# Paired projections from seven block products, with their sums on VectorE, in a hybrid RG-LRU / HGRN2 / MoE layer

## What is computed

```python
def token_mixer(h, s_lru, s_hgrn, row_len, lb, w_in, ...):
    proj = h @ w_in                                   # (tokens x 1024) @ (1024 x 3584)
    xr, gr, q_raw, ff, fb, iv, og = jnp.split(proj, ...)     # seven groups of 512 columns
    y_lru = rmsnorm(h_f + h_b, norm_lru) * jax.nn.gelu(gr)   # two RG-LRU scans of conv(xr)
    y_hg, new_hgrn = hgrn2(q_raw, ff, fb, iv, og, lb, norm_hgrn, s_hgrn)
    y = jnp.concatenate([y_lru, y_hg], axis=-1) @ w_out

def hgrn2(...):                       # four heads of 128 channels, two directions each
    q = silu(q_raw) * DK ** -0.5;  v = i_raw
    # direction: logf = log(lb + (1-lb) sigmoid(f)), k = (1-lb) sigmoid(-f); gated chunks with a state
    o = rmsnorm(o_f + o_b, gain) * silu(g_raw)
```

## Time and profile before

| | us |
|---|---|
| median of three runs | 959.01 |
| the profiled execution | 958.34 |
| its span | 956.6 |
| TensorE busy | 928.8 (97%) |
| VectorE busy | 516.9 (54%) |
| ScalarE busy | 289.7 (30%) |
| GpSimd busy | 101.2 (11%) |

### The profile page before, as it was taken

The page is one execution under the profiler, slowest core; times in us unless marked ns, Lnnn a source line. Parts: engine busy times, 40 slices in busy tenths (PEclk is TensorE's granted clock), DMA queues, the critical chain, the costliest instruction groups (busy, mean ns, idle before and its releaser), DMA issues.

```text
span 956.6 us, 19027 instructions
## 1 busy us (share of the span) xinstructions
PE 928.8 (97%) x8298; PEld 423.3 (44%) x8298; DVE 516.9 (54%) x1269; ACT 289.7 (30%) x507; POOL 101.2 (11%) x115
## 2 busy tenths in 40 slices
PE   5999999999999999999999999999999999999996
PEld 4555756768667554463222222222222223333332
DVE  4487667663654743764464461752636516444096
ACT  5137756564653824323020100200202002010103
POOL 3200010000000022112102002011020110100100
PEclk9999999999999999999999999999999999999999
DMA  9991014404029443168999999999999999999993
GB/s 333 334 386 52 2 55 157 160 5 176 10 92 367 174 164 150 66 240 323 403 399 404 408 416 408 415 401 413 418 405 413 405 413 425 401 426 413 412 380 122
DMA packets 52930, 276.15 MB, mean 289 GB/s; under 512 B 4400, under 2 KB 12752, under 8 KB 39920
## 3 DMA queue, kind: packets, MB, share of 16 engines
q1 hardware_dynamic: 45744, 253.77, 66.1%
q0 software_dynamic: 5584, 15.89, 5.7%
q10 hardware_dynamic: 1520, 5.28, 1.4%
HBM read 261.91 MB, written 13.01 MB: 287 GB/s over the span
## 4 chain that ended last, share of the span: by engine, by line
PE 79%; DMA 8%; DVE 5%; ACT 3%; issue 3%; POOL 0%; SPq 0%; POOLq 0%; DVEq 0%; ACTq 0%
PE pa L699 44%; PE p L699 34%; DMA ring<-in_w_up_dram 3%; DMA reg_e<-in_w_up_dram 3%; DMA ring<-in_w_ada_dram 1%; ACT reg_c L1374 1%; ACT L1374 1%; ACT reg_d L1374 1%; DMA reg_c<-h_rows,row_s 0%; ACT reg_b L1374 0%; DVE reg_a L2246 0%; DVE reg_b L1867 0%; PE p L854 0%; DVE reg_a L2241 0%; DVE reg_b L1838 0%
## 5 line engine op out<-in xcount | busy, mean ns | idle before, releaser
L699 PE MATMUL pa<-ring,reg_b 128*32 128x512 f32 (+1 forms) x1696 | 250.0, 593 | 0.7 <-DMA ring<-in_w_up_dram 0.5
L699 PE MATMUL p<-ring,reg_b 128*16 128x512 f32 (+1 forms) x1920 | 215.3, 592 | 1.1 <-issue 1.1
L699 PE MATMUL pa<-reg_a,ring 128*128 128x512 f32 (+1 forms) x640 | 191.2, 453 | 2.2 <-DVE reg_a L1730 1.5
L699 PEld LDWEIGHTS pa<-ring,reg_b 128*32 128x32 f32 (+1 forms) x1696 | 82.5, 117 | 143.7 <-issue 142.6
L699 PEld LDWEIGHTS pa<-reg_a,ring 128*128 128x128 f32 x640 | 98.3, 191 | 80.1 <-issue 79.9
L699 PEld LDWEIGHTS p<-ring,reg_b 128*16 128x16 f32 (+1 forms) x1920 | 63.9, 102 | 143.9 <-issue 143.9
L2142 DVE STREAM_TRANSPOSE reg_b<-reg_b 32x128 f32<-32x128 f32 x384 | 116.3, 303 | 5.9
L2158 DVE TENSOR_TENSOR reg_b<-reg_b,pa 128x512 f32<-128x512 f32 x16 | 11.0, 686 | 146.7 <-PE pa L699 146.4
L1374 ACT ACTIVATE reg_b<-pa 128x512 f32<-128x512 f32 (+1 forms) x20 | 12.4, 619 | 239.8 <-PE pa L699 239.8
L1374 ACT ACTIVATE reg_b<-reg_d,x_mod 128x128 f32<-128x128 f32 (+1 forms) x112 | 39.4, 440 | 140.7 <-PE p L699 140.7
L1374 ACT ACT_TABLE_LOAD x57 | 73.1, 1283 | 4.6 <-issue 2.8
(11 more groups left out here) (335 smaller groups left out, 937.4 us busy)
## 6 DMA issues: line engine op xcount, KB each, us to landing
ring<-in_w_gate_dram SPq DMA_DIRECT2D x25, 2048.0 KB, 21.1
ring<-in_w_down_dram SPq DMA_DIRECT2D x24, 2048.0 KB, 24.1
ring<-in_w_up_dram SPq DMA_DIRECT2D x22, 2048.0 KB, 21.5
ring<-in_w_ada_dram SPq DMA_DIRECT2D x8, 2048.0 KB, 8.5
ring<-in_w_in_dram SPq DMA_DIRECT2D x6, 2048.0 KB, 19.9
ring<-in_w_ada_dram SPq DMA_DIRECT2D x8, 1024.0 KB, 12.8
reg_a<-in_w_up_dram SPq DMA_DIRECT2D x4, 2048.0 KB, 20.3
reg_a<-in_w_gate_dram SPq DMA_DIRECT2D x3, 2048.0 KB, 18.1
```

Of the source, the lines that this page charges most:

```text
L699: return nc.tensor.matmul(out, lhsT, rhs, start=start, stop=stop, **kw)
```

## The change

Items 0 and 1 of the last two of each `FILL[u]`, u = 0 to 5, become a pair in `TWOS`: (Q, OG), (FF, FB) of heads 1, 2 and 3. A pair's product, [1024 x 256] weights with 640 tokens, is cut in 2 x 2 blocks on each side (512 rows; 320 tokens, `HALF`), and computed by seven block products (a scheme of Strassen and Winograd) instead of eight: each `product` is four matmuls of 320 columns.

- Token sums `x_sum`: four [128 x 1280] sums, once, by GpSimd. Weight sums `weight_sums`: four [128 x 512] sums for each pair by VectorE, two pairs ahead.
- The products go to four PSUM banks. ScalarE copies two of them (`two_copy`); seven adds of 320 columns on VectorE join them (`two_sum`, step 0 in every unit between `less` and `weigh`; steps 1 to 4, six adds, after `reach` in even units and after the state copy in odd ones). In even units ScalarE then runs Silu over both results, in place.
- TensorE's order in a unit is new (`unit_projections`); `EARLY` is now V of head 1; V of heads 2 and 3 comes first in its unit. `head_norm` moves behind the fourth product.
- `w_in` arrives in cells of 1024 x 128 (0.5 MB, runs of 512 bytes) in the order of their use; the sums take the place of two ring slots. Some slots are freed later. A few buffers and semaphores are renamed or moved; GpSimd's store of the LRU state comes behind its sums.

```diff
 
 
 LOADS = [(("ada", 0), 0), (("in", IN_XR), 4), (("ada", 1), 1), (("ada", 2), 2), (("ada", 3), 3),
-         (("in", IN_Q), 5), (("in", IN_OG), 0), (("in", IN_FF), 1), (("in", IN_FB), 2), (("in", IN_V), 3)]
+         (("head", 5), 5), (("head", 0), 0), (("head", 1), 1), (("sums", 0), 2), (("sums", 1), 3)]
 LOADS += [(("ada", c), 4) for c in range(4, 12)] + [(("in", IN_GR), 4), (("out", 0), 5), (("out", 1), 0)]
...
+    FILL += [[(IN_Q, _h), (IN_OG, _h)], ([(IN_V, _h)] if _h > 1 else []) + [(IN_FF, _h), (IN_FB, _h)]]
+TWOS = [fill[-2:] for fill in FILL]
 FILL += [[(IN_GR, 0), (IN_GR, 1)], [(IN_GR, 2), (IN_GR, 3)]]
-HEAD0 = [(IN_Q, 0), (IN_OG, 0), (IN_FF, 0), (IN_FB, 0), (IN_V, 0)]
-
-EARLY = FILL[1].pop(0)
+
...
+        mixing = ring[:, 2:4, :, :].rearrange("p s k n -> p (s k n)")
+        x_sum = [mixing[:, m * 4 * HALF:(m + 1) * 4 * HALF].rearrange("p (k t) -> p k t", k=4) for m in range(4)]
+        w_sum = [[mixing[:, 16 * HALF + (3 * b + m) * 512:16 * HALF + (3 * b + m + 1) * 512].rearrange("p (k n) -> p k n", k=4)
+                  for m in range(3)] for b in range(2)]
+        x_quarter = [[hT[:, 4 * kh:4 * kh + 4, HALF * th:HALF * (th + 1)] for kh in range(2)] for th in range(2)]
+        banks = [pa[n // 2][:, 512 * (n % 2):512 * (n % 2) + HALF] for n in range(4)]
...
+            def cell_load(g, h):
+
+                src = w_in_v[:, :, g * 512 + h * P:g * 512 + (h + 1) * P]
+                sp_eng.dma_start(w_cell((g, h)), src).then_inc(loaded[CELL_BY[(g, h)][0]], 16)
...
+                cell_load(g, 0)
+            sp_eng.wait_ge(freed[0], 1)
+            cell_load(IN_V, 0)
+            cell_load(IN_Q, 1)
+            cell_load(IN_OG, 1)
+            cell_load(IN_V, 1)
+            sp_eng.wait_ge(freed[1], 1)
+            cell_load(IN_FF, 1)
+            cell_load(IN_FB, 1)
+            cell_load(IN_Q, 2)
+            cell_load(IN_OG, 2)
+            whole_load("ada", 4)
+            sp_eng.wait_ge(full, 3)
+            cell_load(IN_FF, 2)
+            sp_eng.wait_ge(full, 4)
+            cell_load(IN_FB, 2)
+            sp_eng.wait_ge(full, 5)
+            cell_load(IN_V, 2)
+            sp_eng.wait_ge(full, 6)
+            cell_load(IN_V, 3)
+            whole_load("ada", 5)
+            whole_load("ada", 6)
+            sp_eng.wait_ge(two_ps, 7)
+            sp_eng.wait_ge(*cells_by((IN_V, 3)))
+            cell_load(IN_Q, 3)
+            cell_load(IN_OG, 3)
...
+            pool.wait_ge(freed[2], 1)
+            pool.wait_ge(freed[3], 1)
+            nc.gpsimd.tensor_tensor(x_sum[0], x_quarter[1][0], x_quarter[1][1], ALU.add).then_inc(mixed, 1)
+            nc.gpsimd.tensor_tensor(x_sum[2], x_quarter[0][0], x_quarter[1][0], ALU.subtract).then_inc(mixed, 1)
+            pool.wait_ge(mixed, 2)
+            nc.gpsimd.tensor_tensor(x_sum[1], x_sum[0], x_quarter[0][0], ALU.subtract).then_inc(mixed, 1)
+            pool.wait_ge(mixed, 3)
+            nc.gpsimd.tensor_tensor(x_sum[3], x_quarter[0][1], x_sum[1], ALU.subtract).then_inc(mixed, 1)
...
+            def product(i, bank, w, x):
+                for k in range(4):
+                    r = mm(banks[bank], w[:, k, :], x[:, k, :], k == 0, k == 3)
+                r.then_inc(two_ps, 1)
+
+            def two_start(i):
+
+                one, two = TWOS[i]
+                for g, h in (one, two):
+                    pe.wait_ge(*cells_by((g, h)))
+                pe.wait_ge(empty[0], (USE[one] + 1) // 2)
+                product(i, 0, w_cell(one)[:, 0:4, :], x_quarter[0][0])
+                pe.wait_ge(empty[1], USE[one] // 2)
+                pe.wait_ge(mixed, 4)
+                pe.wait_ge(two_add, weights_by(i))
+                product(i, 2, w_sum[i % 2][0], x_sum[0])
+
+            def two_middle(i):
+
+                product(i, 1, w_cell(TWOS[i][0])[:, 4:8, :], x_quarter[0][1])
+
+            def two_second(i):
+
+                product(i, 3, w_sum[i % 2][1], x_sum[1])
+
+            def two_third(i):
+
+                pe.wait_ge(two_cp, copied_by(i) + 2)
+                product(i, 2, w_cell(TWOS[i][1])[:, 4:8, :], x_sum[3])
+                product(i, 0, w_cell(TWOS[i][1])[:, 0:4, :], x_sum[2])
+
+            def two_last(i):
+
+                pe.wait_ge(two_add, joined_by(i) + 1)
+                product(i, 3, w_sum[i % 2][2], x_quarter[1][1])
+                pe.sem_inc(full, 2)
+                for at, slots in ((2, (1,)), (4, (5,)), (5, (0, 2, 3))):
+                    if i == at:
+                        pe.wait_ge(two_ps, 7 * i + 7)
+                        for s in slots:
...
+            def unit_projections(u):
+                if len(FILL[u]) > 2:
+                    project(FILL[u][0])
+                if u > 0:
+                    two_start(u)
+                if u == 1 or u == 3 or u == 5:
+                    pe.wait_ge(sc_done, NSC * u)
+                    ada_sum(ADA_UNIT[u])
+                two_middle(u)
                 if u == 0:
                     pe.wait_ge(ln_log, 1)
-                elif u in ADA_UNIT:
-                    pe.wait_ge(sc_done, NSC * u)
-                if u in ADA_UNIT:
                     ada_sum(ADA_UNIT[u])
-                project_prompt(fill[0])
+                two_second(u)
+                if u == 2 or u == 4:
+                    head_norm(u // 2 - 1)
+                two_third(u)
+                if u == 2 or u == 4:
+                    turn_k(u)
+                    two_last(u)
+                    return
+                if u <= 1:
+                    ada_sum(ADA_UNIT[u] + 1)
+                    turn_k(u)
+                    two_last(u)
+                else:
+                    two_last(u)
+                    ada_sum(ADA_UNIT[u] + 1)
+                    turn_k(u)
+                ada_turn(ADA_UNIT[u])
...
+            def two_copy(i, step):
+                (one_a, one_b), (two_a, two_b) = two_out(TWOS[i][0]), two_out(TWOS[i][1])
+                act.wait_ge(two_ps, 7 * i + 1 + step)
+                A((one_a, two_b)[step], banks[2 * step], ACT.Copy).then_inc(two_cp, 1)
...
                 chain(A(kk, f, ACT.Sigmoid, scale=-1.0))
                 A(lf, W[6], ACT.Ln, bias=lb[:, 4 * d + h:4 * d + h + 1], scale=oml[:, 4 * d + h:4 * d + h + 1]).then_inc(lfk, 1)
+                if len(fill) > 2:
+                    projected(fill[0])
+                if u < len(TWOS):
+                    two_copy(u, 0)
+                    two_copy(u, 1)
...
+                elif d == 0:
+                    for item in fill:
+                        n = USE[item]
+                        act.wait_ge(empty[n % 2], n // 2 + 1)
+                    for item in fill:
+                        dst = yT[:, LT + item[1], :] if item[0] == IN_OG else raw[item[1] % 2][2]
+                        A(dst, dst, ACT.Silu).then_inc(two_cp, 1)
...
+            def weight_sums(i):
+                one, two = TWOS[i]
+                for item in (one, two):
+                    dve.wait_ge(*cells_by(item))
+                if i >= 2:
+                    dve.wait_ge(two_ps, 7 * (i - 1))
+                t1, t2, t4 = w_sum[i % 2]
+                a, b, at = w_cell(one), w_cell(two), weights_by(i) - 4
+                V.tensor_tensor(t1, b[:, 0:4, :], a[:, 0:4, :], ALU.subtract).then_inc(two_add, 1)
+                V.tensor_tensor(b[:, 0:4, :], b[:, 4:8, :], b[:, 0:4, :], ALU.subtract).then_inc(two_add, 1)
+                dve.wait_ge(two_add, at + 1)
+                V.tensor_tensor(t2, b[:, 4:8, :], t1, ALU.subtract).then_inc(two_add, 1)
+                dve.wait_ge(two_add, at + 3)
+                V.tensor_tensor(t4, a[:, 4:8, :], t2, ALU.subtract).then_inc(two_add, 1)
+
...
             V.memset(reg_e[:, 0:2 * T], 0.0).then_inc(zeroed, 1)
 
             for j in range(1, LT):
...
+            def two_sum(i, step):
+                (one_a, one_b), (two_a, two_b) = two_out(TWOS[i][0]), two_out(TWOS[i][1])
+                at = joined_by(i)
+                if step == 4:
+                    for dst, other in ((two_a, two_b), (two_b, one_b)):
+                        dve.wait_ge(two_add, at + (4 if dst is two_a else 5))
+                        V.tensor_tensor(dst, dst, other, ALU.add).then_inc(two_add, 1)
+                after, dst, src, bank = ((4, two_a, one_a, 3), (3, one_a, one_a, 1), (6, one_b, two_a, 0),
+                                         (5, two_a, two_a, 2), (7, one_b, one_b, 3))[step]
+                dve.wait_ge(two_ps, 7 * i + after)
+                if step == 0:
+                    dve.wait_ge(two_cp, copied_by(i) + 1)
+                else:
+                    dve.wait_ge(two_add, at + (6 if step == 4 else step))
+                V.tensor_tensor(dst, src, banks[bank], ALU.add).then_inc(two_add, 1)
+                if step == 2 or step == 4:
+                    dve.wait_ge(two_add, at + (7 if step == 4 else step + 1))
+                    dve.sem_inc(empty[step // 4], 1)
 
...
                     less(W[lv], 2 * hs, hs - 1 + d)
+                if u < len(TWOS):
```

(58 more changed lines are left out.)

114 lines of the change are left out of this document (74 added, 40 removed).

## The result

| | before | after |
|---|---|---|
| median | 959.21 us (6 runs, 957.84 to 960.46) | 980.85 us (6 runs, 979.27 to 985.72) |
| the profiled execution, its span | 958.34, 956.6 | 979.6, 977.9 |
| TensorE busy | 928.8 us (97%) | 922.3 us (94%) |
| VectorE busy | 516.9 us | 558.7 us |
| first projection of head 0 starts | 69.65 | 77.12 |

The ratio is 1.023, 95% interval 1.0205 to 1.0255: slower by 21.6 us, where I had forecast 11.6 and a range up to 976. Of the 21.3 us between the two spans 21.0 are there by the end of unit 6; what follows takes the same time in both. So the question is the stretch from 50 to 344 us.

A forecast was written before the change was run, and what follows sets the result against it. TensorE's queue was taken as the bound: new waits of 26.2 us, less 1.4 of present waits and a 13.2 us gain, make +11.6, so 970.5 us against the 959.01 median. The range for 8 in 10 was 961 to 976.

The forecast's parts named there:

- The gain: TensorE's six pairs of projections: 15.12 us a pair instead of 17.31, 13.2 us less in all.
- copies of unit 0 behind `lru_y`: Unit 0: ScalarE's two new copies stand behind the late LRU norm and logarithm, so TensorE waits 4.7 us.
- scores 0 on the bias behind the joins: Unit 0: VectorE issues ada's bias add behind the joins, so TensorE waits 4.3 us before the scores.
- outputs, units 1, 3, 5: Joins delay the masked copies that the output sums need: TensorE waits 2.6, 2.6 and 3.9 us.
- keys, units 2, 4: `head_norm` moves back, so ScalarE's exponentials and `k_tok` come later: TensorE waits 1.6 us in each unit.
- V of head 3 on the joins of unit 4: Unit 4: joins delay VectorE's last weighing, whose buffer V of head 3 needs: TensorE waits 1.4 us.
- The step that failed: GpSimd's four token sums, from about 50 to 62 us: 12.0 us long, needed 60 us later, counted as costing nothing.
- lock-out: GpSimd's sums hold VectorE's convolution off through shared ports; the tile up to 12 us later, TensorE waiting up to 7.4 us.
- slower still, up to 978: Rival at the LRU convolution: the lock-out adds up to 7.4 us to the forecast; chance 0.08.
- joins nearly free: Rival at VectorE's joins: a dependent add takes 0.2 us instead of 0.52, giving 961 us; chance 0.09.
- faster: Rival at VectorE's joins: its lateness never reaches TensorE, all 14.8 us of join waits go, giving 955.7; chance 0.06.
- the gain isn't there: Rival at TensorE's passes of 320 columns: weight loads hold them to 0.30 us, giving 977 us; chance 0.03.

The follow-up runs named there:

- changed_again: The changed kernel, unaltered, run once more for a second trace: 980.27 us.
- late_joins: The changed kernel with the last four joins of units 1, 3 and 5 moved behind the masked copies and the sums of both ways: 983.66 us.
- sums_on_vector: The changed kernel with the four token sums on VectorE, in its idle time before the first and third gates' squares, instead of GpSimd: 973.74 us.
- bias_and_load_first: The changed kernel with unit 0's ada bias sum ahead of its last four joins and ada 7's load ahead of head 3's last two cells: 977.39 us.
- bias_first: The changed kernel with unit 0's ada bias sum on VectorE ahead of the last four joins of unit 0: 982.4 us.

## Why the prediction was wrong, point by point

**The gain** was right: 2.155 us a product ((204.88-200.57)/2), 15.1 for a pair instead of the 17.31 of before, 13.3 us in all (forecast 13.2).

**The waits** were right within a few tenths each, and a little too high together:

| | forecast | measured |
|---|---|---|
| copies of unit 0 behind `lru_y` | 4.7 | 4.19 |
| scores 0 on the bias behind the joins | 4.3 | 3.01 |
| outputs, units 1, 3, 5 | 2.6, 2.6, 3.9 | 2.22, 2.23, 3.60 |
| ada's second load | 0.3 (unit 1) | 0 (unit 1), 0.45 (unit 5) |
| `ada_turn`, units 3, 5 | 1.1, 1.1 | 0.96, 0.96 |
| copy of V, unit 3 | 1.0 | 0.89 |
| keys, units 2, 4 | 1.6, 1.6 | 1.51, 1.51 |
| V of head 3 on the joins of unit 4 | 1.4 | 1.92 |
| sum | 26.2 | 23.5 |

The adds took 0.485 us each, and the four last steps of unit 1 take 3.4 us together (VectorE's timeline), where I had 0.52 and 3.3:

```profile
190.62 1.07 DVE L2098 TENSOR_TENSOR reg_d<-reg_d,pa 128x320 f32<-128x320 f32 x2
191.91 0.49 DVE L2098 TENSOR_TENSOR reg_d<-reg_d,pa 128x320 f32<-128x320 f32 x1 [0.21 <-DVE reg_d L2098]
192.43 1.02 DVE L2090 TENSOR_TENSOR reg_d<-reg_d 128x320 f32<-128x320 f32 x2
193.55 0.49 DVE L2098 TENSOR_TENSOR reg_d<-reg_d,pa 128x320 f32<-128x320 f32 x1
```

The term for scores 0 looks like the one most mis-sized, 3.0 for 4.3. But TensorE comes to it later by what half clock costs the products ahead of it, and the two together are the forecast wait: 1.5 us lost with a wait of 3.0, in changed_again 2.4 with 2.2, in late_joins 2.6 with 1.9, in sums_on_vector 1.7 with 2.8, each time 4.5 or 4.6. So at full clock the waits would be 25.0 us for my 26.2. With this, bias_and_load_first, where no wait stands behind that stretch, has 3.3 us less than the changed kernel beside the clock (261.6 + 1.5 - 259.8), just what the expectation of bias_first said.

**The step that failed** is the one at GpSimd's sums: "needed 60 us later: nothing" was said of TensorE's need, and of the meeting with VectorE "I take nothing, and the other end is a rival". The rival was the case. I had a bound of 7.4 us with no row for or against it, and took the end that suited the sum; it should have been the likeliest case, as the sentence that I had cited spoke for it and no row against it. Measured: head 0's projections 7.5 us later, 0.5 of it from the start of the execution, 2.5 of it half clock. My "if it held VectorE off for all of 12.0 us" was too much: the tile ended 8.9 us later, since the first sum ran before the convolution began. The Trainium skill ("SBUF — State Buffer", section "SBUF: two separate sides") says that whichever of the two starts first has the shared pair of ports for its whole instruction, where VectorE's has two inputs in SBUF or is in a mode with two ports. The trace agrees for two inputs: such an operation was held to 3.40 us. A TENSOR_SCALAR with one tensor as input was held to 2.91; no row tells its mode.

**The term that was missing** is the clock. I read 1.00 in the kernel before and took it as given for a TensorE that stands still 24 us more. The loss is 4.8 us within units 0 to 6 of the first trace, 7.4 in the second; 3.3 and 5.0 of it add to the time, the rest shortens the wait before scores 0.

The sum, at the end of unit 6: start of the execution 0.5, lock-out with its half clock 6.9, waits 25.0 at full clock less 1.6 of before (0.41 and four of 0.30; the 0.6 more that I had counted at the outputs of unit 5 stands in no row of waits), gain -13.3, half clock in the units 3.3: 20.8 us, the trace has 21.0. Without the lock-out and the clock it is 10.6 with the start, near my 11.6; they are 10.2 together. My range had 5.5 us above the forecast, enough for the clock but not for the lock-out: without the latter, in sums_on_vector, the time is 973.7 and within the range.

**What I had said would show it**: TensorE's busy time falls by 6.5, not 13 us, since half clock fills 7 us of it; the waits bear the names I gave; unit 1 ends at 197.67, 8.2 us behind the forecast 189.5, of which 7.5 were there when head 0 started; the convolution ends after 70 us, the sign I had named for the lock-out. The rival "slower still, up to 978" had the mechanism of the lock-out and nearly its size; the measured 980.85 lies past it by the clock. The others fail on rows: "joins nearly free" on the adds (0.485 us, not 0.2), "faster" on the waits for VectorE at the outputs (8.1 us), "the gain isn't there" on the passes (0.269 us, not 0.30). Even with joins of one column the kernel stays 14 us slower than before.

## What to carry to other kernels

Work given to an idle engine isn't free if it holds up another engine's queue that runs beside it: look for what it meets, and give it to the busy engine in a gap that the timeline shows (four sums of 1.5 us in VectorE's idle time cost nothing, four of 3 us on GpSimd cost 7). When a change turns work of the bounding engine into waits, a wait costs more than its length: here 24 us of waits brought 5 to 7 us of half clock with them, 3 to 5 of which added to the time. And before a wait is removed, look what it hides: a load at 2.9 to 4.2 us, and `head_norm` at 9.6, took back what two of the edits had won.
